# A two-block transformer kernel: grouped-query stage laid out anew, probabilities scaled before transposing, last feed-forward by tokens

## Chip, cores and metric

One core of a Trainium2 chip runs the whole program. The metric is device time in microseconds of one execution, lower is better. Times before are three executions; the profile is of one more.

## The reference, cut to what matters

```
x: (1, 256, 1024) float32
x = x + mixed(rms_norm(x)) @ w_out           # stick-breaking attention, conv, ssm
x = x + cross_attention(rms_norm(x), mem)     # 4 heads of 256
x = x + swiglu(rms_norm(x))                   # feed-forward 0, hidden 2816
x = x + [latent attention (8 heads), dilated attention (3 groups x 4)] @ w_out_ab
x = x + swiglu(rms_norm(x))                   # feed-forward 1
q = rope(rmsnorm(h @ w_q)); k = rope(rmsnorm(h @ w_k)); v = h @ w_v    # 16 q heads, 4 kv heads of 64
x = x + softmax(q k^T / 8) v @ w_o            # grouped-query stage
x = x + swiglu(rms_norm(x))                   # feed-forward 2
return rmsnorm(x, final_norm)                 # y = x * rsqrt(mean(x^2) + eps) * gain
```

## The kernel before

x stays on chip as `xT`, features on partitions, 8 tiles of 128x256. Each engine has its own instruction stream, written out by hand in order, and semaphores tie them together: an engine does its work strictly in the order written. All weights come in pieces of 128x2048 float32 (1 MB) through three `raw` buffers. ACT copies a piece to `whi` in a reduced float32 form, half a piece at a time, and DVE subtracts to get the rest, `wlo` (L764 and L1337 outside the feed-forwards, L1140 and L1722 inside). `split` does one such half; `after(name, idx)` does the splits of the piece whose buffer tile (name, idx) has freed. Each product of a projection is three matmuls: hi x hi, hi x lo, lo x hi (L1949 to L1951 with weights stationary, L2009 to L2011 and L2500 with activations stationary).

A projection tile takes 24 matmuls of 256 columns into one of four PSUM banks in turn (`Plan.tile`, `ring_bank`); `claim` waits until the earlier tile of the same bank is evacuated. Helper `plain` (L2015) issues unsplit float32 matmuls, each of which the profile shows as two records; `pe.transpose` (L2616, L2646) shows as one.

Attention: PE makes scores, DVE takes row maxima, ACT exponentiates and sums, PE turns the probabilities, ACT copies them out, PE multiplies by values, ACT and DVE split the result in hi and lo. In `attend` (cross and latent attention) and in the dilated attention DVE writes a diagonal matrix of reciprocal sums into `hf` (L1702, L1880), and PE turns and scales in one plain float32 matmul against it. In `attend_pairs` (grouped-query) DVE scales the probabilities of two heads (L1330 after L1925) and PE uses `pe.transpose`.

Grouped-query stage: two key tiles are projected side by side, then eight query tiles, each followed in PE's order by the sum of squares of the pair before (`sum_squares`, inside the pair) and by the rotation product (`g_swapped`) of that pair; DVE does for each pair splits, the rotation of the pair before, mean square, scaling (`g_norm`). The value tiles come last, then the last rotation, and only then the first scores; before the first turn PE issues 14 matmuls that nobody reads (`keep_clock`, 28 records).

Feed-forward: a chunk is 256 of 2816 hidden channels. `hidden` makes gate and up (pairs of L2376, 512 columns, and L2378, 256 columns, 16 pairs per half chunk), `output` multiplies a half chunk by its w_out rows into banks 4 to 7 (24 matmuls of 256 columns). Before the first chunk of each, `add_residual` adds the eight tiles of the projection before to xT on DVE, ACT and DVE split the normed x, POOL adds the squares (L732 to L738), and `norm_sum` sums them on PE. After feed-forward 2 the tiles are added to xT, multiplied by the final gain (`final`), squared, summed by columns, transposed to tokens, scaled and stored by one DMA of 1 MB.

## Time and profile before

| what | us |
|---|---|
| median of 3 runs (lowest, highest) | 1214.98 (1212.34, 1221.14) |
| profiled execution, its own time | 1219.0 |
| span from first to last instruction in it | 1217.0 |
| PE busy in it | 1142.1 |
| DVE busy | 836.9 |
| ACT busy | 621.9 |

The profile is of a separate execution, whose own time is 4.0 us over the median of the three; 2.0 us of its time lie outside its span. Busy time of PE is the union of its pipelined matmuls, so that a busy PE may still be given work faster. What is read in it are places: where PE waited, for whom, and the rate at which it worked where it didn't wait.

### The profile page before, as it was taken

The numbers are of one execution on the slowest core, as the hardware profiler recorded it, in microseconds if no ns is written. First come the engines' busy times: TensorE is split into PE (matmuls) and PEld (weight loads), VectorE is DVE, ScalarE is ACT, GpSimd is POOL, SyncE is SP. The second block draws the span as 40 slices with busy tenths as digits, with TensorE's granted clock in tenths as the row PEclk, the third lists the DMA queues.
The fourth block names the chain that finished last, engine by engine and source line by source line (L and its number), as shares of the span: only waits on it lengthen the run. The fifth ranks groups of instructions, "written<-read, shape, count | busy, mean of one in ns | idle before, by whom it ended". The sixth has DMA issues, their size and how long they took to land.

```text
span 1217.0 us, 20958 instructions
## 1 busy us (share of the span) xinstructions
PE 1142.1 (94%) x8064; PEld 1022.6 (84%) x8064; DVE 836.9 (69%) x1291; ACT 621.9 (51%) x1106; POOL 39.5 (3%) x40
## 2 busy tenths in 40 slices
PE   4899899898999999999999989999988799999998
PEld 4787678798989999999977879999987678999997
DVE  3685674456378787777466378787876667778784
ACT  4633445545455455565354455454564565555453
POOL 2000000010010000010000010000010001000000
PEclk8898899999999999999999999999999899999998
DMA  8342222326165567646421056567586205567650
GB/s 256 105 139 82 92 71 69 104 70 190 53 212 175 168 182 207 182 152 201 133 88 35 29 163 178 163 194 207 174 166 143 71 11 166 175 169 206 192 153 36
DMA packets 218145, 169.20 MB, mean 139 GB/s; under 512 B 20787, under 2 KB 208098, under 8 KB 217954
## 3 DMA queue, kind: packets, MB, share of 16 engines
q1 hardware_dynamic: 216962, 164.44, 46.2%
q0 software_dynamic: 496, 2.43, 0.6%
q10 hardware_dynamic: 624, 1.44, 0.4%
q8 instruction: 46, 0.75, 0.3%
q14 instruction: 17, 0.14, 0.0%
HBM read 167.24 MB, written 1.05 MB: 138 GB/s over the span
## 4 chain that ended last, share of the span: by engine, by line
PE 77%; DVE 11%; ACT 7%; issue 2%; SPq 1%; DMA 1%; POOL 0%; POOLq 0%; DVEq 0%; ACTq 0%
PE bank L2376 19%; PE bank L2015 14%; PE bank L1949 10%; PE bank L1950 10%; PE bank L1951 10%; PE bank L2378 10%; DVE wlo L1337 4%; ACT whi L764 2%; DVE arena L1330 2%; PE bank L2009 1%; PE bank L2010 1%; PE bank L2011 1%; ACT arena L1285 1%; SPq L695 1%; DVE hf L1348 1%
## 5 line engine op out<-in xcount | busy, mean ns | idle before, releaser
L2376 PE MATMUL bank<-mem_pair,whi 128*128 128x512 f32 x1056 | 376.4, 399 | 2.5 <-DVE mem_pair L1647 1.6
L2378 PE MATMUL bank<-mem_pair,wlo 128*128 128x256 f32 x1056 | 296.5, 281 | 0.0
L1949 PE MATMUL bank<-act_hi,whi 128*128 128x256 f32 (+1 forms) x920 | 266.0, 289 | 12.7 <-DVE act_lo L1356 4.7
L1950 PE MATMUL bank<-act_lo,whi 128*128 128x256 f32 (+1 forms) x920 | 262.6, 285 | 0.0
L1951 PE MATMUL bank<-act_hi,wlo 128*128 128x256 f32 (+1 forms) x920 | 262.2, 285 | 0.0
L2376 PEld LDWEIGHTS bank<-mem_pair,whi 128*128 128x128 f32 x1056 | 198.5, 188 | 49.6 <-DVE mem_pair L1647 2.7
L1337 DVE TENSOR_TENSOR wlo<-raw,whi 128x1024 fp32r<-128x1024 f32 (+3 forms) x137 | 163.3, 1234 | 103.8 <-ACT whi L764 102.6
L1722 DVE TENSOR_TENSOR wlo<-raw,whi 128x1024 fp32r<-128x1024 f32 x177 | 208.8, 1220 | 4.0
L2378 PEld LDWEIGHTS bank<-mem_pair,wlo 128*128 128x128 f32 x1056 | 199.6, 189 | 0.1
L1949 PEld LDWEIGHTS bank<-act_hi,whi 128*128 128x128 f32 (+1 forms) x920 | 176.8, 192 | 23.7 <-issue 13.0
L1140 ACT ACTIVATE whi<-raw 128x1024 fp32r<-128x1024 f32 x180 | 179.9, 1046 | 0.4 <-PE bank L1951 0.4
L1950 PEld LDWEIGHTS bank<-act_lo,whi 128*128 128x128 f32 (+1 forms) x920 | 177.2, 193 | 0.8 <-issue 0.7
L1951 PEld LDWEIGHTS bank<-act_hi,wlo 128*128 128x128 f32 (+1 forms) x920 | 177.2, 193 | 0.0
L1155 ACT ACTIVATE arena<-arena 128x256 f32<-128x256 f32 x66 | 27.6, 418 | 253.7 <-DVE arena L1330 253.7
L2015 PE MATMUL bank<-arena 32*32 32x256 f32 (+9 forms) x1052 | 134.3, 387 | 17.7 <-ACT arena L1285 4.9
L1746 DVE TENSOR_REDUCE arena<-bank 128x256 f32<-128x512 f32 x132 | 90.6, 686 | 75.8 <-PE bank L2378 75.8
L764 ACT ACTIVATE whi<-raw 128x1024 fp32r<-128x1024 f32 (+3 forms) x134 | 129.5, 1018 | 18.1 <-PE bank L1951 18.1
L2015 PEld LDWEIGHTS bank<-arena 32*32 32x32 f32 (+5 forms) x1052 | 82.7, 136 | 54.3 <-issue 13.2
L1330 DVE TENSOR_TENSOR arena<-arena 128x256 f32<-128x256 f32 (+5 forms) x190 | 95.3, 503 | 40.3 <-ACT arena L1159 21.3
L1949 PE MATMUL bank<-mem_pair,whi 128*128 128x256 f32 (+1 forms) x352 | 106.2, 302 | 2.2 <-DVE mem_pair L1647 2.2
L1950 PE MATMUL bank<-mem_pair,whi 128*128 128x256 f32 (+1 forms) x352 | 101.0, 287 | 0.0
L1951 PE MATMUL bank<-mem_pair,wlo 128*128 128x256 f32 (+1 forms) x352 | 100.8, 286 | 0.0
(216 smaller groups left out, 1330.4 us busy)
## 6 DMA issues: line engine op xcount, KB each, us to landing
raw<-in_ffn_w_in_dram SPq DMA_DIRECT2D x132, 512.0 KB, 5.1
raw<-in_ffn_w_out_dram SPq DMA_DIRECT2D x33, 1024.0 KB, 5.0
raw<-in_w_in_ab_dram SPq DMA_DIRECT2D x11, 1024.0 KB, 5.4
raw<-in_w_in_dram SPq DMA_DIRECT2D x9, 1024.0 KB, 6.2
raw<-in_xa_wk_dram SPq DMA_DIRECT2D x4, 1024.0 KB, 5.7
raw<-in_xa_wv_dram SPq DMA_DIRECT2D x4, 1024.0 KB, 5.2
raw<-in_w_out_dram SPq DMA_DIRECT2D x4, 1024.0 KB, 5.2
raw<-in_xa_wq_dram SPq DMA_DIRECT2D x4, 1024.0 KB, 5.2
```

What stands on the lines that cost most here:

```text
L764: act.activation(whi[g % SLOTS][:, h * n:h * n + n], raw[g % SLOTS][:, h * n:h * n + n], ACT.Copy)\
L1140: act.activation(whi[slot][:, h * 1024:h * 1024 + 1024], raw[slot][:, h * 1024:h * 1024 + 1024], ACT.Copy).then_inc(s_split_hi, 1)
L1330: return dve.tensor_tensor(dst, a, b, ALU.mult)
L1337: dve.tensor_tensor(wlo[g % SLOTS][:, at_], raw[g % SLOTS][:, at_], whi[g % SLOTS][:, at_].bitcast(F32), ALU.subtract).then_inc(s_split_lo, 1)
L1722: dve.tensor_tensor(wlo[slot][:, at_], raw[slot][:, at_], whi[slot][:, at_].bitcast(F32), ALU.subtract)\
L1746: dve.tensor_reduce(x[:, j, :], bank[2 * j + g][:].rearrange("p (h t) -> p t h", h=2), AX.X, ALU.add)\
L1949: pe.matmul(dst, w[0], a[0], start=start, stop=False, **kw)
L1950: pe.matmul(dst, w[0], a[1], start=False, stop=False, **kw)
L1951: return pe.matmul(dst, w[1], a[0], start=False, stop=stop, **kw)
L2015: return pe.matmul(dst, w, a, start=start, stop=stop, skip_group_check=True)
L2376: pe.matmul(b[:].rearrange("p (h t) -> p h t", h=2), w[0][:, k, g, :], mem_pair[:, :, k, :], start=k == 0, stop=False, skip_group_check=True)
L2378: last = pe.matmul(b[:, 0:T], w[1][:, k, g, :], mem_hi[:, k, :], start=False, stop=k == KC - 1, skip_group_check=True)
```

## The change

The diff has some 900 lines. It does the following.

1. Grouped-query stage. The tiles get banks by name, six in all (0 to 3, 5, 6). The sums of squares and rotation products are issued from hooks inside later query tiles. The key pair's squares and the x statistics are taken while the first query tile runs; the first scores come before the value projection, `g_sum(4)` and `g_swapped(3)` lie inside the two value tiles, and `g_swapped(4)` behind the third scores. `keep_clock` is gone. DVE does the last scaling and two rotations between attention steps; the splits for gqa_wo 1 and 2 move to the end of, and behind, the attention.
2. Cross, latent and dilated attention: DVE multiplies the probabilities by the reciprocal sums in place (128x512 at once, or 128x768 twice for the dilated one), and PE uses `pe.transpose`. In cross attention the last query pair is normed inside the first attention steps, and its piece's split comes behind the attention; so does the split after the latent value tiles, behind the dilated attention.
3. `add_residual` and `residual_in` leave the splits after tiles 5 and 7 to the end in all four places (before in one).
4. Feed-forwards: in the first chunk the first half's hi and lo of the hidden come before the splits.
5. Feed-forward 2 works by tokens in its down projection: `x_by_tokens` puts x into banks 4 to 7 (16 plain 128x128 matmuls against the identity), and `output_tokens` accumulates 12 matmuls of 512 columns per half chunk with the hidden stationary. ACT squares and sums each bank, makes the scale, DVE multiplies by it and by the gain, three DMAs store. The final gain is loaded late by POOL, broadcast to 128 partitions (512 KB written), and no longer with the rows at the start.

```diff
-    p.tile("gk", 0, "dve")
-    p.tile("gk", 1, "dve", ("gkv", 0))
-    for j in range(4):
+    p.tile("gk", 0, "dve", None, 0)
+    p.tile("gk", 1, "dve", ("gkv", 0), 1)
+    for j, (b0, b1) in enumerate(((2, 3), (5, 6), (0, 1), (2, 3))):
         p.piece(("gq", j))
-        p.tile("gq", 2 * j, "dve")
-        p.tile("gq", 2 * j + 1, "dve", ("gq", j))
+        p.tile("gq", 2 * j, "dve", None, b0)
+        p.tile("gq", 2 * j + 1, "dve", ("gq", j), b1)
     p.piece(("gkv", 1))
-    p.tile("gv", 0, "act")
-    p.tile("gv", 1, "act", ("gkv", 1))
+    p.tile("gv", 0, "act", None, 5)
+    p.tile("gv", 1, "act", ("gkv", 1), 6)
     residual(p, "gqa_wo")
...
-            sp.wait_ge(s_fine, 4)
-            sp.dma_start(out[0].rearrange("(t p) d -> p t d", p=P), y_tok).then_inc(s_store, 16)
-            sp.wait_ge(s_store, 16)
+            by_token = out[0].rearrange("(t p) d -> p t d", p=P)
+            sp.wait_ge(s_fine, 2)
+            sp.dma_start(by_token[:, 0, :], y_tok[:, 0, :]).then_inc(s_store, 16)
+            for half in range(2):
+                sp.wait_ge(s_fine, 3 + half)
+                at_ = slice(512 * half, 512 * half + 512)
+                sp.dma_start(by_token[:, 1, at_], y_tok[:, 1, at_]).then_inc(s_store, 16)
+            sp.wait_ge(s_store, 48)
 
...
+            pool.dma_start(final_gain, ins["final_norm_2"].rearrange("(a n) -> a n", a=1).to_broadcast([P, D])).then_inc(s_gain, 16)
...
-            rms_from(("xq", 3))
-            after("xq", 7)
...
-            attend(0, 4, probs, probsT, XA_UNITS)
-            residual_in(3, "xa_wo")
+            attend(0, 4, probs, probsT, XA_UNITS, lambda: rms_from(("xq", 3)))
+            after("xq", 7)
+            residual_in(3, "xa_wo", (5, 7))
             x_rms_of(3)
...
+                        early = first and j == 0
+                        if early:
+                            hidden_hi(i, j)
...
-            ffn_tail(1, 6)
+            ffn_tail(1, 6, lambda: pair_squares("gk", "g", 0, 4, split_last=False))
             x_rms_of(6)
-
-
-            for i, j in enumerate(G_ORDER):
-                pair_squares("gq" if j < 4 else "gk", "g", 2 * j if j < 4 else 0, j,
-                             (("g", G_ORDER[i - 1]), 512) if i else None)
-            rms_from(("g", G_ORDER[-1]), 512)
+            rms_from(("g", 4), 512)
+            after("gk", 1)
             x_rms_columns(6)
-            for i in range(2):
-                evacuate("gv", i, gv[:, i, :], scale=x_rms_col[:, i, 0:1])
+            for i in range(1, 5):
+                if i > 1:
+                    rms_from(("g", G_ORDER[i - 1]), 512)
+                pair_squares("gq", "g", 2 * i - 2, G_ORDER[i], split_last=i < 4)
+
+            def gv_out(t):
+
+                evacuate("gv", t, gv[:, t, :], scale=x_rms_col[:, t, 0:1], follow=False)
+
             def attend_pairs(first, pairs):
 
                 for i in range(pairs + 3):
+                    if i == 1:
+                        rms_from(("g", G_ORDER[4]), 512)
+                        gv_out(0)
+                        after("gq", 7)
+                        gv_out(1)
                     for half in range(2):
...
-            act.wait_ge(s_ss, SQ["norm", 8] + 4)
-            step(act.activation(x_rms_col[:], bank[4][:, 0:4].rearrange("p (t k) -> p t k", t=2), ACT.Ln,
-                                scale=1.0 / D, bias=eps[:, 0:1]))
-            act.activation(x_rms_col[:], x_rms_col[:], ACT.Exp, scale=-0.5).then_inc(s_col, 1)
-            act.wait_ge(s_col, 3)
+
+
             for t in range(TT):
-                act.wait_ge(s_fint, 2)
-                act.activation(y_tok[:, t, 0:512], bank[2 * t][:], ACT.Copy, scale=x_rms_col[:, t, 0:1]).then_inc(s_fine, 1)
+                for half in range(2):
+                    act.wait_ge(s_fin, 2 * t + half + 1)
+                    act.activation(sq[:, half, :], bank[4 + 2 * t + half][:], ACT.Square,
+                                   accum_out=final_sums[:, t, half:half + 1]).then_inc(s_mean, 1)
+                act.wait_ge(s_mean, 4 * t + 1)
+                act.activation(final_scale[:, t, :], final_sums[:, t, 0:1], ACT.Identity, scale=1.0 / D, bias=eps[:, 0:1])\
+                   .then_inc(s_mean, 1)
+                act.wait_ge(s_mean, 4 * t + 3)
+                act.activation(final_scale[:, t, :], final_sums[:, t, 1:2], ACT.Ln, scale=1.0 / D, bias=final_scale[:, t, :])\
+                   .then_inc(s_mean, 1)
+                act.wait_ge(s_mean, 4 * t + 4)
+                act.activation(final_scale[:, t, :], final_scale[:, t, :], ACT.Exp, scale=-0.5).then_inc(s_scale, 1)
...
-                        for t in range(TT):
-                            last = dve.tensor_scalar(rescale(a, t), ident, rsum[:, a, t:t + 1], None, ALU.mult)
-                        last.then_inc(s_p, 1)
+                        mul(probs_[:, a % 2, :, :], probs_[:, a % 2, :, :],
+                            rsum[:, a, :].unsqueeze(2).to_broadcast([P, TT, T])).then_inc(s_p, 1)
+                    if middle is not None:
+                        middle(i)
                     if i >= 4 and out_units[i - 4] is not None:
...
-                dve.wait_ge(s_dexp, 2 * s + 2)
-                step(dve.reciprocal(rsum[:, 28 + s, :], rsum[:, 28 + s, :]))
                 for t in range(TT):
-                    last = dve.tensor_scalar(dil_rescale(s, t), ident, rsum[:, 28 + s, t:t + 1], None, ALU.mult)
-                last.then_inc(s_dp, 1)
+                    dve.wait_ge(s_dexp, 2 * s + t + 1)
+                    step(dve.reciprocal(rsum[:, 28 + s, t:t + 1], rsum[:, 28 + s, t:t + 1]))
+                    d = dprobs2[:, s % 2, t, :]
+                    dve.tensor_scalar(d, d, rsum[:, 28 + s, t:t + 1], None, ALU.mult).then_inc(s_dp, 1)
...
+            g_mean(0)
+            g_scaled(0)
+            after("gk", 1)
+            for i in range(1, 4):
+                g_mean(i)
+                after("gq", 2 * i - 1)
+                g_scaled(i)
+                g_rotate(i - 1)
+
             def attend_pairs(first, pairs):
 
+                def scale_pair(a):
+
+                    dve.wait_ge(s_exp, a + 2)
+                    step(dve.reciprocal(rsum[:, a:a + 2, :], rsum[:, a:a + 2, :]))
+                    pr = gprobs[:, a % 4:a % 4 + 2, :, :].rearrange("p h l m -> p (h l) m")
+                    r = rsum[:, a:a + 2, :].rearrange("p h l -> p (h l)")
+                    mul(pr, pr, r.unsqueeze(2).to_broadcast([P, 2 * TT, T])).then_inc(s_p, 2)
+
                 for i in range(pairs + 4):
+                    if i == 1:
+                        g_mean(4)
+                        scale_pair(first)
+                        g_scaled(4)
+                        g_rotate(3)
                     if i < pairs:
                         for a in range(first + 2 * i, first + 2 * i + 2):
                             dve.wait_ge(s_score, a + 1)
...
-                    if 1 <= i <= pairs:
-                        a = first + 2 * i - 2
-                        dve.wait_ge(s_exp, a + 2)
-                        step(dve.reciprocal(rsum[:, a:a + 2, :], rsum[:, a:a + 2, :]))
-                        pr = gprobs[:, a % 4:a % 4 + 2, :, :].rearrange("p h l m -> p (h l) m")
-                        r = rsum[:, a:a + 2, :].rearrange("p h l -> p (h l)")
-                        mul(pr, pr, r.unsqueeze(2).to_broadcast([P, 2 * TT, T])).then_inc(s_p, 2)
+                    if 2 <= i <= pairs:
+                        scale_pair(first + 2 * i - 2)
+                    if i == 2:
+                        g_rotate(4)
                     if i >= 4:
                         c = i - 4
                         dve.wait_ge(s_ohi, OHI[8 + c])
                         dve.tensor_tensor(act_lo[:, c, :], bank[6 + c % 2][:, 0:T], act_hi[:, c, :].bitcast(F32),
                                           ALU.subtract).then_inc(s_olo, 1)
+                    if i == pairs:
+                        after("gq", 7)
 
             attend_pairs(12, 8)
+            after("gv", 1)
             add_residual("gqa_wo", 7)
...
-            dve.wait_ge(s_col, 3)
+            dve.wait_ge(s_gain, 16)
             for t in range(TT):
-                dve.wait_ge(s_fint, 2)
-                dve.tensor_scalar(y_tok[:, t, 512:D], bank[2 * t + 1][:], x_rms_col[:, t, 0:1], None, ALU.mult)\
-                   .then_inc(s_fine, 1)
+                dve.wait_ge(s_scale, t + 1)
+                for half in range(2):
+                    at_ = slice(512 * half, 512 * half + 512)
+                    dve.scalar_tensor_tensor(y_tok[:, t, at_], bank[4 + 2 * t + half][:], final_scale[:, t, :],
+                                             final_gain[:, at_], ALU.mult, ALU.mult).then_inc(s_fine, 1)
 
 
...
-                                last = plain(turned_bank(a)[:, m * T + l * P:m * T + l * P + P],
-                                             probs_[:, a % 2, l, m * P:m * P + P], rescale(a, l))
+                                last = pe.transpose(turned_bank(a)[:, m * T + l * P:m * T + l * P + P],
+                                                    probs_[:, a % 2, l, m * P:m * P + P], ident)
...
+                def output_tokens(j, value, hidden_value, end=False):
+
+                    pe.wait_ge(s_split_lo, value)
+                    pe.wait_ge(s_fflo, hidden_value)
+                    w = [x[os_][:, j * D:j * D + D] for x in (whi, wlo)]
+                    for t in range(TT):
+                        for half in range(2):
+                            b, of, to = bank[4 + 2 * t + half], slice(t * P, t * P + P), slice(512 * half, 512 * half + 512)
+                            plain(b[:], hid_hi[:, j, of], w[0][:, to], False, False)
+                            plain(b[:], hid_hi[:, j, of], w[1][:, to], False, False)
+                            last = plain(b[:], hid_lo[:, j, of], w[0][:, to], False, end)
+                            if end:
+                                last.then_inc(s_fin, 1)
+                    if not end:
+                        last.then_inc(tile_done, 1)
+
+                def x_by_tokens():
+
+                    pe.wait_ge(s_rms, 2 * stat_no["norm", n] + 1)
+                    for c in range(KC):
+                        for t in range(TT):
+                            at_ = slice((c % 4) * P, (c % 4) * P + P)
+                            plain(bank[4 + 2 * t + c // 4][:, at_], xT[:, c, t * P:t * P + P], ident, c % 4 == 0, False)
+
+                step = output_tokens if f == 2 else output
+
                 def chunk(i, first=False, last=False):
...
-            for i, j in enumerate(G_ORDER[1:]):
-                for k in range(2):
-                    project("gq", 2 * j + k, ("gq", j), P * k, XN)
-                    if k == 0:
-                        if i == 0:
-                            norm_sum(6)
-                        sum_squares(("g", G_ORDER[i]), 0, bank[4][:], 2, True, True, blocks)
-                        if i == 1:
-                            x_rms_columns(6)
-                g_swapped(i)
-            for t in range(TT):
-                project_tokens("gv", t, ("gkv", 1), t, XN)
-                if t == 0:
-                    sum_squares(("g", G_ORDER[-1]), 0, bank[4][:], 2, True, True, blocks)
-            g_swapped(4)
+            GQ_HOOKS = ({4: lambda: g_sum(0), 6: lambda: norm_sum(6)}, {4: lambda: x_rms_columns(6)},
+                        {4: lambda: g_sum(1)}, {4: lambda: g_swapped(0)},
+                        {4: lambda: g_sum(2)}, {4: lambda: g_swapped(1)},
+                        {4: lambda: g_sum(3)}, {4: lambda: g_swapped(2)})
+            for n in range(8):
+                project("gq", n, ("gq", n // 2), P * (n % 2), XN, hooks=GQ_HOOKS[n])
...
-                if tile == 0:
-                    evac_wait(pe, "gv", 1)
+                if tile < 2:
+                    evac_wait(pe, "gq", 5 + 2 * tile)
...
-                            keep_clock(SOFTMAX_FILL, 6)
+                            g_swapped(4)
+                            evac_wait(pe, "gv", 1)
...
+            gqa_scores(0, (score_bank(12), score_bank(13)))
+            project_tokens("gv", 0, ("gkv", 1), 0, XN, hooks={4: lambda: g_sum(4)})
+            project_tokens("gv", 1, ("gkv", 1), 1, XN, hooks={2: lambda: g_swapped(3)})
```

## Rows read from the trace of the kernel before

**Rows 1.** Part 2 of the page: TensorE's granted clock in 40 slices.

```profile
PEclk8898899999999999999999999999999899999998
```

**Rows 2.** Busy by stretch: length, PE, PEld, DVE, ACT, POOL, clock.

```profile
687.00:722.00 35.00, 31.44 (x219) 28.28 (x218) 23.35 (x37) 18.07 (x29) 5.49 (x4) 1.00 0.40 121
908.00:959.00 51.00, 39.83 (x268) 32.71 (x268) 34.95 (x48) 25.19 (x48) 0.00 (x0) 0.99 0.62 151
959.00:991.00 32.00, 28.86 (x207) 20.47 (x208) 20.70 (x35) 23.69 (x80) 0.00 (x0) 0.91 0.01 2
```

**Rows 3.** Timeline of PE in the third feed-forward (start us, us, what).

```profile
1106.74 0.40 PE L2376 MATMUL bank<-mem_pair,whi 128*128 128x512 f32 x1
...
1112.38 0.28 PE L1949 MATMUL bank<-act_hi,whi 128*128 128x256 f32 x1
...
1115.26 0.40 PE L2376 MATMUL bank<-mem_pair,whi 128*128 128x512 f32 x1
```

**Rows 4.** The chain that ended last, at the latent value projection.

```profile
627.40 2.74 PE bank L2500 x12
```

**Rows 5.** Timeline of PE, cross attention ([idle before it <- what ended it]).

```profile
303.53 2.08 PE L2015 MATMUL bank<-hf,arena 128*128 128x128 f32 x8 [3.67 <-DVE hf L1702]
...
308.81 1.20 PE L2015 MATMUL bank<-hf,arena 128*128 128x128 f32 x8
```

**Rows 6.** Timeline of DVE at the same place.

```profile
298.74 2.36 DVE L1337 TENSOR_TENSOR wlo<-raw,whi 128x1024 fp32r<-128x1024 f32 x2
```

**Rows 7.** Timeline of PE, latent attention, two heads.

```profile
638.52 1.06 PE L2015 MATMUL bank<-hf,arena 128*128 128x128 f32 x8
639.50 2.14 PE L2015 MATMUL bank<-arena 128*64 128x256 f32 x8
641.48 1.06 PE L2015 MATMUL bank<-hf,arena 128*128 128x128 f32 x8
```

**Rows 8.** Timeline of PE, dilated attention, slots 0 and 1.

```profile
658.45 3.00 PE L2015 MATMUL bank<-hf,arena 128*128 128x128 f32 x24 [1.42 <-DVE hf L1880]
...
666.90 3.00 PE L2015 MATMUL bank<-hf,arena 128*128 128x128 f32 x24
```

**Rows 9.** Timeline of PE, entries of the second and third feed-forward.

```profile
708.17 0.51 PE L2376 MATMUL bank<-mem_pair,whi 128*128 128x512 f32 x1 [1.61 <-DVE mem_pair L1647]
...
712.60 0.70 PE L2015 MATMUL bank<-x_sum,ones 128*128 128x256 f32 x2 [1.00 <-POOL x_sum L738]
...
1027.06 0.36 PE L1949 MATMUL bank<-act_hi,whi 128*128 128x256 f32 x1 [0.89 <-DVE act_lo L1767]
```

**Rows 10.** Timeline of PE, grouped-query stage.

```profile
917.28 1.13 PE L2015 MATMUL bank<-arena 128*128 128x512 f32 x2 [2.18 <-DVE arena L1348]
...
958.81 2.08 PE L2015 MATMUL bank<-arena 64*128 64x256 f32 x8 [4.92 <-ACT arena L1285]
960.82 5.12 PE L2015 MATMUL bank<-ones 128*128 128x128 f32 x28
...
972.32 1.06 PE L2616 MATMUL bank<-cst,arena 128*128 128x128 f32 x8
973.32 2.15 PE L2015 MATMUL bank<-arena 128*64 128x256 f32 x16
975.61 0.63 PE L2616 MATMUL bank<-cst,arena 128*128 128x128 f32 x4
```

**Rows 11.** Groups by line, 966 to 985 us (busy us, mean ns of one).

```profile
L1285 ACT ACTIVATE arena<-bank,nmax 128x256 f32<-128x256 f32 x24 | 11.0, 471 | 6.7 <-PE bank L2616 6.3
...
L1330 DVE TENSOR_TENSOR arena<-arena,rsum 128x1024 f32<-128x1024 f32 x5 | 6.1, 1225 | 0.5
L1294 ACT ACTIVATE arena<-bank 128x512 f32<-128x512 f32 x11 | 6.1, 611 | 0.0
```

**Rows 12.** The chain from the last down projection on.

```profile
1203.77 0.87 PE bank L2015 x8
```

**Rows 13.** SP's waits in the last 17 us.

```profile
SPq L286 <- DMA out_dram<-arena: 3.6, 1, 3.6
```

More of the change, by code:

```diff
@@ L68, in __init__ @@
         self.bank_no = {}
+        self.bank = {}
         self.evac = {}
@@ L2598, in attend_pairs @@
             def attend_pairs(first, pairs):
-                for i in range(pairs + 3):
+                for i in range(1, pairs + 3):
                     if i < pairs:
```

196 lines of the change are left out of this document (102 added, 94 removed).

## The prediction, made before the result was known

> **What bounds the kernel now.** I read the granted clock by slices first, then the busy table by stretch, then PE's timeline where its busy share falls, and at each gap what ended it. The clock is near its upper level (2.4 GHz; the lower is 1.2) nearly everywhere [rows 1]. In the feed-forwards PE has no gap. Its rate there is seen from starts, since the records overlap: 16 pairs of hidden take 1112.38 - 1106.74 = 5.64 us, 0.353 a pair, and 24 matmuls of 256 columns take 2.88 us, 0.120 each [rows 3]. So the kernel is bound by PE's stream, and time can be saved in three ways: fewer or cheaper PE instructions, gaps removed between stages, and the tail after the last projection. The gaps are large in the grouped-query stage: 51.0 us with 39.8 busy, then 32 us at a mean clock of 0.91 [rows 2]. The whole span has 1217.0 - 1142.1 = 75 us without PE.
>
> **Price of a turn.** A plain 128x128 float32 matmul costs 0.98 / 4 = 0.245 us (a head's four, from 638.52 to 639.50 [rows 7]). Eight transposes take 973.32 - 972.32 = 1.00 us, 0.125 each [rows 10]. So four turns fall from 0.98 to 0.50 us.
>
> **Grouped-query stage.** PE's idle before: 11.2 us in 908 to 959 [rows 2], of which 2.2 wait for the scaled keys and 4.9 for the first exponentials [rows 10]. Removed in attention: keep_clock, 965.8 - 960.8 = 5.0 us at the lower clock; 1.0 us since the scores before it (958.81 to 960.82) took twice what 8 such records take in 1.0; and about 1.2 us of waiting right behind. That is 18.4 us at most. What comes in place, going through the new order: the key squares are taken at about 909.3 before the ACT split, so the first sum fits into query tile 0. ACT then has a split (2.0), the x statistics (1.4), the key's Ln and Exp (1.3) and another split before the squares of the first query pair, which are ready some 0.8 us after PE asks for them in tile 2; later hooks have slack (about 1.5 us each; a split pair on DVE is 2.4 [rows 6]). PE's work from the end of the keys to the end of the values is 240 x 0.12 = 28.8, ten sums and rotations at about 0.45, small ones 0.4 and the first scores 1.0, thus about 34.7 us plus 0.8. The first exponentials run under the value tiles. Then the attention is bound by ACT: 972.32 to 975.61 is 3.29 us a pair [rows 10], against four exponentials at 0.45, two copies at 0.5 and an output of 0.4, 3.2 us; DVE has two maxima (1.3), reciprocal and scaling (0.3 + 1.2) and one low part (0.4), also 3.2 [rows 11]. Into this full DVE queue the change puts g_rotate(4), 2.2 us, while ACT's next exponentials wait: I charge 1.5. The split for gqa_wo 1 on DVE at the end (2.4) delays the last low parts by 0.2. gqa_wo 2 is split behind the attention, and covered by four projection tiles of 2.9 us; without that cover it would cost its 2.4. Sum: 18.4 - 0.8 - 1.5 - 0.2 = 15.9; following the order gives 17.2. I take 16.5, with bounds 9 and 19.
>
> **Cross attention.** PE waits 3.67 us [rows 5], because DVE does a split of 2.36 [rows 6] before it takes the first maxima. That split is moved behind the attention; the last norm goes between maxima. In my order the first turn starts near 299.9 instead of 303.5. Behind this wait the clock was at its lower level: eight turn records last 2.08 us [rows 5], and 1.06 in latent attention [rows 7]. The stretch from 303.53 to 308.81 therefore holds 2.6 us too much. Four heads' turns save 1.9. Against it: DVE's scaling of 128x512 is half of the 128x1024 one, plus overhead, 0.7 instead of 0.5 us, and two waits of some 0.3. Gain 3.6 + 2.6 + 1.9 - 0.7 = 7.4 us; 4 if the clock falls all the same.
>
> **Latent attention.** A head is 641.48 - 638.52 = 2.96 us of unbroken PE [rows 7], turns 0.98 of it. With 0.50 it is 2.5. ACT has two exponentials, a copy and half an output, 0.9 + 0.6 + 0.3 [rows 11]; DVE a maximum 0.7, reciprocal 0.2, scaling 0.7, half a low part 0.2. Both stay at 1.8. The first two turns wait for the scaling, so six or seven heads gain 0.5 each: 3.5. **Dilated attention.** PE waits 1.42 us at its start [rows 8] behind the split that is now moved to the end (on DVE it lies beneath the first tile of w_out_ab; uncovered it would cost 1.8); of that 1.1 goes. A slot is 8.45 us [rows 8], with 24 records of turns, 2.93. Twelve transposes are 1.5, but the third group waits for the copy of the first (two banks): 1.8. Gain 4 x 1.1; DVE's two scalings of 768 take longer than two of 128, which costs in the last slot 0.2, and the moved ACT split 0.4 there. Gain 3.5 + 1.1 + 3.8 = 8.4 us.
>
> **Entries of the feed-forwards.** The second waits 1.6 for the x split and 1.0 for POOL's squares [rows 9], since DVE is held by the splits after tiles 3 and 5. In 687 to 722, the output projection up to the first output matmul, PE shows 35.0 - 31.4 = 3.6 us idle [rows 2]; as a gap begins only when the pipelined matmul before it ends, each of the four costs 0.28 more, 4.7. With the late splits and the early hidden all of it goes, but the first reduction of chunk 0 is then held by the late splits for 0.9: 3.8. The first has one such wait of 0.7 and one before its first output, and gains 1.5. In the third the wait before the first output is 0.89 [rows 9], 1.06 us over PE's step; it goes. What is late next is the second half's hidden: some 1.3 us later, of a slack of 2.6.
>
> **Feed-forward 2 by tokens.** x_by_tokens adds 16 x 0.245 = 3.9 us on PE's path, less the 1.06 gap: +2.9. An output falls from 24 x 0.120 = 2.88 to 12 matmuls of 512. Twelve of that form, activations stationary, took 2.74 [rows 4]; as the wide one of a hidden pair it would be 0.353 - 0.120 = 0.233, 2.80. 22 outputs gain 1.8 to 3.1; I take 2.5. The hidden as stationary needs the same semaphores.
>
> **Tail.** Before, from 1203.77 [rows 12] to the span's end, 13.2 us. After, from the last matmul: two squares of a bank on ACT, the second 0.65 us behind the first, about 1.65; three small steps 0.9; DVE two multiplications 1.4; then a 256 KB store instead of 1 MB. The wait for 1 MB was 3.6 us [rows 13]; a quarter in size gives 0.9 if all is transfer, 3.6 if none; I take 2.1 and 0.4 for the issue. 6.5 us; gain 6.7, bounds 5 and 8. The late gain load (POOL's queue has nothing behind it) has 170 us to land.
>
> **Start.** One row DMA less on SP, whose last landing the chain waits for: 0.3 (0 to 0.6).
>
> **Sum** against the profiled execution's 1219.0: 16.5 + 7.4 + 8.4 + 3.8 + 1.5 - 2.9 + 2.5 + 6.7 + 0.3 = 44.2, so 1174.8. The median is 4.0 lower: 1171.
>
> **A rule against it.** In grouped-query attention, a third of whose PE work is transposes, the clock came back and stayed high: after about 965 us no fall is seen until the tail [rows 1, 2]. The Trainium skill says (TensorE: Matmul & The Clock Gate, Part 4: PE-mode transpose) that transposes don't count as PE activity for the clock. If the clock fell for that, each stage with turns would run at half. By the rows the sum stands.
>
> **Rivals.**
> (a) The grouped-query stage keeps half its waits: DVE and ACT do their lists strictly in order, and with splits of 2.4, rotations of 2.2 and scalings of 0.9 a round, one late hook passes on to the next. For it: DVE is filled to 3.2 of 3.29 us in attention. Against: a projection pair lasts PE 6.7 us, and DVE's round is 6.2. Then the gain there is 9: 1179. Chance 0.20.
> (b) The cheaper turns only uncover DVE: exponentials, then scaling, then turn, in latent, cross and dilated attention; 8.4 + 1.9 give 4: 1177. Against: PE has 2.5 us a head, DVE 1.8. Chance 0.12.
> (c) Slower: transposes let the clock fall in cross, latent and dilated attention and in the grouped one. PE's 48 us of latent and dilated work would cost 48 more, cross 8, grouped 20: 1247. It decides from 44 us of lost time on, nearly all those stages. Chance 0.03.
> (d) The order doesn't take effect since the landing of weights sets the pace: gqa_w_q pieces have 256-byte runs. They had landed by 910 before, needed at 915. Gain left only in tail and turns, 15 or less: 1200 to 1208; chance 0.03.
> The forecast has 0.62. The range reaches 8 lower, where the order in grouped-query works out fully (19), tail 8 and outputs 3.1, and to 1188, (a) and (b) together with the low tail: 1161 to 1188. Within 1% is about what a measurement can tell from nothing. Faster by over 1%: 0.94; within: 0.03; slower 0.03.
>
> **What would show it.** PE's rows in the stage of the grouped queries: no gap over 1 us from the keys to the first turn; 3.3 us a pair after. A latent head at 2.5 us, a slot at 7.3. First output of each feed-forward without a gap; output in chunks of feed-forward 2 near 2.75. The tail 6.5 us. I'd be wrong by a clock at its lower level in any attention stage, by PE waiting for DVE's scalings, or by a pair period above 3.5.

## The result and the profile after

The changed kernel takes 1175.15 us (median of 4, 1169.1 to 1177.42), the kernel before 1214.35 in the same comparison: a ratio of 0.966, 95% interval 0.9607 to 0.9713. The forecast was 1171 in a range of 1161 to 1188. The profiled execution took 1177.42 us, its span 1175.3, so that it stands 41.7 under the profiled one before (44.2 forecast).

Cut at the first PE record of each stage, the two traces give this (us; "forecast" is the sum of the terms of the prediction for the stage):

| stage | before | after | measured | forecast |
|---|---|---|---|---|
| mixing, up to the first cross scores (not changed, but for one load) | 293.65 | 295.57 | +1.92 | -0.3 |
| cross attention, to xa_wo | 24.83 | 16.90 | -7.93 | -7.4 |
| xa_wo and feed-forward 0 | 214.01 | 213.33 | -0.68 | -1.5 |
| projections of latent and dilated | 92.95 | 92.95 | 0 | 0 |
| latent attention, to the first dilated turn | 33.01 | 28.67 | -4.34 | -4.6 |
| dilated attention | 28.81 | 24.95 | -3.86 | -3.8 |
| w_out_ab and feed-forward 1 | 211.16 | 207.57 | -3.59 | -3.8 |
| grouped-query stage, to gqa_wo | 92.23 | 75.78 | -16.45 | -16.5 |
| gqa_wo and feed-forward 2, to its last matmul | 212.96 | 212.71 | -0.25 | +0.4 |
| tail | 13.39 | 6.87 | -6.52 | -6.7 |

This table is the instrument of all that follows. In the 14 profiled executions of this study the projection stage, which no kernel changed, lasted 92.93 to 92.96 us, while the mixing stage lasted 287.56 to 297.31. The mean clock of the first 287 us was 0.92 in the profile after, 0.93 before and 0.95 in the run `gqa_only` below. Most of the spread between executions sits there, in falls of the clock. Where the clock doesn't fall, a stage length tells differences of 0.1 to 0.2 us. Where it falls it tells less: cross attention in its old form took 24.83, 24.83, 24.86 and 25.10 us in four profiles, the old tail 11.43 to 13.39. A median of whole executions doesn't tell 2.

The granted clock after (part 2 of the page) shows the same; what answers to [rows 1] has its falls in the first 10 slices and none behind:

```profile
PEclk8998889989999999999999999999999999999999
```

The grouped-query stage by stretch (length, PE, PEld, DVE, ACT, POOL, clock), against [rows 2]: first keys to first scores, then scores and values to gqa_wo. The clock, 0.91 before in the attention, is 1.00 in both.

```profile
879.94:919.00 39.06, 37.73 (x268) 33.18 (x268) 29.81 (x44) 24.05 (x42) 4.72 (x4) 1.00 0.85 180
919.00:955.72 36.72, 32.60 (x241) 22.65 (x239) 30.90 (x50) 29.48 (x93) 0.00 (x0) 1.00 0.10 20
```

PE's timeline after (start us, us, what, idle before):

```profile
301.63 0.66 PE L2387 MATMUL bank<-cst,arena 128*128 128x128 f32 x4
302.51 1.97 PE L2080 MATMUL bank<-arena 128*128 128x256 f32 x8 [0.22 <-DVE arena L1371]
...
357.05 0.36 PE L2009 MATMUL bank<-act_hi,whi 128*128 128x256 f32 x1 [0.30 <-DVE act_lo L1770]
...
628.62 0.60 PE L2387 MATMUL bank<-cst,arena 128*128 128x128 f32 x4
629.16 2.14 PE L2080 MATMUL bank<-arena 128*64 128x256 f32 x8
631.13 0.60 PE L2387 MATMUL bank<-cst,arena 128*128 128x128 f32 x4
...
711.20 0.36 PE L2009 MATMUL bank<-act_hi,whi 128*128 128x256 f32 x1 [0.20 <-DVE act_lo L1770]
...
926.77 3.05 PE L2080 MATMUL bank<-arena 64*128 64x256 f32 x18
929.66 1.04 PE L2709 MATMUL bank<-cst,arena 128*128 128x128 f32 x8
930.65 1.13 PE L2080 MATMUL bank<-arena 64*128 64x256 f32 x8
933.05 1.06 PE L2709 MATMUL bank<-cst,arena 128*128 128x128 f32 x8 [1.26 <-ACT arena L1312]
934.04 2.15 PE L2080 MATMUL bank<-arena 128*64 128x256 f32 x16
937.39 1.06 PE L2709 MATMUL bank<-cst,arena 128*128 128x128 f32 x8 [1.20 <-ACT arena L1312]
...
940.67 1.06 PE L2709 MATMUL bank<-cst,arena 128*128 128x128 f32 x8
...
991.22 3.73 PE L2080 MATMUL bank<-cst,xT 128*128 128x128 f32 x32
994.70 0.47 PE L2080 MATMUL bank<-whi,act_hi 128*128 128x512 f32 x1
...
1003.19 0.40 PE L2080 MATMUL bank<-whi,act_hi 128*128 128x512 f32 x1
...
1005.94 0.39 PE L2441 MATMUL bank<-mem_pair,whi 128*128 128x512 f32 x1
```

To be seen in it: the wait of [rows 5] ahead of the first cross turn is gone. A latent head is 631.13 - 628.62 = 2.51 us ([rows 7]: 2.96). The gap before the first output of each feed-forward is gone, but in the first two feed-forwards a small one stands before the second output (357.05, 711.20). A pair of grouped-query heads takes 940.67 - 937.39 = 3.28, except for one of 4.34 (933.05 to 937.39); that one is over the 3.5 which the prediction named as a sign of being wrong. The rotation that it had charged for makes it (run 4). An output by tokens is 2.75 (1003.19 to 1005.94), x_by_tokens 3.48.

### The profile page after: what moved, and what is told of

It reads as the page before. It is cut to its first block, busy times and chain, and to the rows that moved or that the text cites. A ratio compares the mean times of both kernels' runs of the same rounds, so it can differ in the third digit from the quotient of the medians.

```text
span 1175.3 us, 20129 instructions
## 1 busy us (share of the span) xinstructions
PE 1118.8 (95%) x7660; PEld 988.1 (84%) x7660; DVE 839.6 (71%) x1277; ACT 618.3 (53%) x1104; POOL 39.2 (3%) x41
## 3 DMA queue, kind: packets, MB, share of 16 engines
HBM read 167.76 MB, written 1.05 MB: 144 GB/s over the span
## 4 chain that ended last, share of the span: by engine, by line
PE 80%; DVE 9%; ACT 7%; issue 2%; SPq 1%; DMA 1%; POOLq 0%; POOL 0%; DVEq 0%; ACTq 0%
PE bank L2441 19%; PE bank L2080 17%; PE bank L2009 10%; PE bank L2443 10%; PE bank L2010 9%; PE bank L2011 9%; DVE wlo L1360 2%; DVE arena L1353 2%; PE bank L2074 2%; PE bank L2076 2%; PE bank L2075 2%; ACT whi L766 1%; SPq L691 1%; ACT arena L1303 1%; DVE wlo L1756 1%
## 5 line engine op out<-in xcount | busy, mean ns | idle before, releaser
L2009 PE MATMUL bank<-act_hi,whi 128*128 128x256 f32 (+1 forms) x744 | 216.5, 291 | 10.5 <-DVE act_lo L1379 4.7
L2010 PE MATMUL bank<-act_lo,whi 128*128 128x256 f32 (+1 forms) x744 | 212.9, 286 | 0.0
L2011 PE MATMUL bank<-act_hi,wlo 128*128 128x256 f32 (+1 forms) x744 | 212.8, 286 | 0.0
L2009 PEld LDWEIGHTS bank<-act_hi,whi 128*128 128x128 f32 (+1 forms) x744 | 143.8, 193 | 20.5 <-issue 13.2
L2010 PEld LDWEIGHTS bank<-act_lo,whi 128*128 128x128 f32 (+1 forms) x744 | 144.0, 193 | 0.8 <-issue 0.7
L2011 PEld LDWEIGHTS bank<-act_hi,wlo 128*128 128x128 f32 (+1 forms) x744 | 144.0, 194 | 0.0
```

The costliest lines, as they stand in the source:

```text
L2009: pe.matmul(dst, w[0], a[0], start=start, stop=False, **kw)
L2010: pe.matmul(dst, w[0], a[1], start=False, stop=False, **kw)
L2011: return pe.matmul(dst, w[1], a[0], start=False, stop=stop, **kw)
```

## Experiments

Each is compared by stage with the kernel that it was made from; the ratio is to the kernel before.

**1. The grouped-query stage alone** (`gqa_only`: banks, hooks, order and missing keep_clock put into the kernel before, nothing else).

> The kernel before with the grouped-query stage of the change alone: tile banks by name, hooks, values behind the first scores, no keep_clock; turns, splits, feed-forwards and tail are as before. Theory A, the stage's gain stands by itself: from the first key tile to gqa_wo's first matmul 75.8 us as in the changed kernel instead of 92.2 (before: 898.42 to 990.65), and about 16.4 us off the time, 1198. Rival B, the new order pays only together with the late splits and the cheaper turns around it: under 12 us in the stage, or more than 2 us given back in the residual addition behind it.

1195.8 us, ratio 0.9854 (0.9826 to 0.9882). The stage is 75.80 us, the stages between it and cross attention are those of before to 0.03. Theory A holds. The tail was 1.96 shorter too, 11.43, with no change made there: the mean clock in it was 0.77, and 0.62 in the profile before. The clock fell 3.2 us into the tail in the profile before, 6.2 us into it here. `no_fill` (run 2) shows the same: tail 11.45, clock 0.83, the fall after 7.5 us. So some 2 us of the 6.5 that the tail shows depend on when the clock falls in the old tail.

**2. What keep_clock was worth** (`no_fill`), **and whether transposes bring the clock back** (`fill_transposes`), both in the kernel before; the added lines are those of the second, the first has none:

```
                         if i == 2:
-                            keep_clock(SOFTMAX_FILL, 6)
+                            for _ in range(2 * SOFTMAX_FILL):
+                                pe.transpose(bank[6][:, 0:P], ones[:], ident)
```

> The kernel before without keep_clock: PE waits for the first probabilities instead of issuing 28 records that nobody reads. Theory A, those records did little there, since the clock was already down when they started (957.6) and stood at the lower level until 964.5: the time falls by 0 to 2 us or stays, and PE waits until DVE's first scaled pair. Rival B, they brought the clock back: without them the turns and values behind run at the lower clock for several us, 2 to 5 us slower.

> The kernel before with 28 transposes in place of the 14 plain matmuls (28 records) of keep_clock, so that PE is given as many records. Theory A, transposes bring the clock back as matmuls do: the granted clock rises at about 965 as before, the pair periods behind stay at 3.29 us, time within 1 us. Rival B, transposes don't count for the clock: it stays low for some us longer, the next turns and values take twice their time, 2 to 6 us slower.

Without it: 0.9981 (0.9957 to 1.0006) as a whole, and 87.97 instead of 92.23 us in the stage, 4.26 less. Theory A has the sign and less than half the size; theory B is out. PE in that run:

```profile
959.11 2.08 PE L2015 MATMUL bank<-arena 64*128 64x256 f32 x8 [4.92 <-ACT arena L1285]
961.12 1.97 PE L2616 MATMUL bank<-cst,arena 128*128 128x128 f32 x8
963.02 2.00 PE L2015 MATMUL bank<-arena 64*128 64x256 f32 x8
964.95 1.09 PE L2616 MATMUL bank<-cst,arena 128*128 128x128 f32 x8
```

The first turn starts at once, so the probabilities were ready when the 28 records began: keep_clock held up ready work. Turns and scores last twice their time until about 964.8, where the granted clock rises, and then their own. So 4.26 is less than the fill's own 4.95 us: the low clock stays, and real work runs under it. With transposes as the fill (ratio 1.0002, 0.9976 to 1.0028; stage 92.18) the rise comes as early. PE's timeline, then its busy time and the granted clock by stretch:

```profile
959.63 5.05 PE L2610 MATMUL bank<-cst,ones 128*128 128x128 f32 x28
964.52 1.04 PE L2617 MATMUL bank<-cst,arena 128*128 128x128 f32 x8
965.49 1.13 PE L2015 MATMUL bank<-arena 64*128 64x256 f32 x8
```

```profile
962.00:963.00 1.00, 1.00 (x7) 0.50 0.00 0
963.00:964.00 1.00, 1.00 (x10) 0.84 0.00 0
964.00:965.00 1.00, 1.00 (x12) 1.00 0.00 0
```

28 transposes and nothing else stood between 959.63 and 964.52. Under them the clock goes from 1.2 GHz (0.50) to 2.4, and the eight turns behind last 1.04 us. The Trainium skill (TensorE: Matmul & The Clock Gate, Part 4: PE-mode transpose) says that the high clock doesn't engage for transposes; these float32 ones did not keep it down.

**3. Values behind the first scores** (`values_first`: that order undone).

```
-            gqa_scores(0, (score_bank(12), score_bank(13)))
             project_tokens("gv", 0, ("gkv", 1), 0, XN, hooks={4: lambda: g_sum(4)})
             project_tokens("gv", 1, ("gkv", 1), 1, XN, hooks={2: lambda: g_swapped(3)})
+            gqa_scores(0, (score_bank(12), score_bank(13)))
```

> The changed kernel with the first grouped-query scores issued behind both value tiles, as the kernel before had them; banks, hooks and the orders of ACT and DVE are unchanged. Theory A, a wait of PE for the first exponentials and scaling returns and the clock falls behind it: 4 to 5.5 us of wait at the first turns, then several us at the lower clock, 6 to 10 us in all. Rival B, the wait returns but the clock stays up, since the transposes and scores around it are dense enough: 4 to 5.5 us and a mean clock above 0.97 through the attention. Rival C, the hooks and banks made the gain and this order made little of it: under 2 us.

1175.52 us, ratio 0.9684 (0.9659 to 0.9709): as a whole not to be told from the changed kernel. The stage says otherwise, 81.97 instead of 75.78 us:

```profile
917.51 1.14 PE L2080 MATMUL bank<-arena 64*128 64x256 f32 x8
923.72 5.44 PE L2080 MATMUL bank<-arena 64*128 64x256 f32 x18 [5.07 <-DVE arena L1371]
928.99 1.04 PE L2709 MATMUL bank<-cst,arena 128*128 128x128 f32 x8
```

A wait of 5.07, and 18 records in 5.44 us that take 3.05 with the clock up (926.77 above). Theory A holds; the mixing stage was 8 us shorter in this execution and hid it. Runs 2 and 3 split the stage's gain: 92.23 without keep_clock 87.97, with banks and hooks 81.97, with the values moved 75.78; 4.26, 6.00 and 6.19 us. These are shares in this order of steps, since the last step also removes the low clock that `no_fill` leaves.

**4. The last rotation** (`rotate_pool`: POOL takes two of its three operations; it is idle there).

```
                     if i == 2:
-                        g_rotate(4)
+                        dve.wait_ge(s_rot, 10)
+                        mul(grot, bank7(P, 2), sin_g.unsqueeze(1).to_broadcast([P, 2, T])).then_inc(s_r4, 1)
...
+            pool.tensor_tensor(x4, x4, cos_g.unsqueeze(1).to_broadcast([P, 2, T]), ALU.mult).then_inc(pool_step, 1)
+            pool.wait_ge(pool_step, 6)
+            pool.wait_ge(s_r4, 1)
+            pool.tensor_tensor(x4, x4, grot, ALU.add).then_inc(s_rd, 1)
```

> The changed kernel with the last query rotation shared: DVE multiplies the rotated half by the sines (0.7 us), POOL does the product with the cosines and the addition, which DVE did in 2 x 0.7. Theory A, this rotation in DVE's full queue is what makes the second pair period of the grouped-query attention 4.34 us instead of 3.28: the period falls to 3.3 to 3.6, the stage from 75.8 to about 75.0, and the next scores that need the rotation come before PE asks for them. Rival B, POOL's two operations slow DVE's own while they run, or end too late for the scores of tile 6: the stage stays at 75.8 or grows.

1171.88 us, ratio 0.9634 (0.9586 to 0.9683); the stage 74.78, 1.00 less. PE, and what POOL's operation did to DVE's scaling:

```profile
933.21 1.06 PE L2718 MATMUL bank<-cst,arena 128*128 128x128 f32 x8 [1.27 <-ACT arena L1320]
934.20 2.15 PE L2089 MATMUL bank<-arena 128*64 128x256 f32 x16
```

```profile
930.13 1.27 POOL L749 TENSOR_TENSOR arena<-arena 128x512 f32<-128x512 f32 x1 [41.70 <-PE bank L2089]
933.23 1.27 POOL L752 TENSOR_TENSOR arena<-arena 128x512 f32<-128x512 f32 x1 [1.83 <-DVE arena L1361]
```

```profile
931.07 1.41 DVE L1361 TENSOR_TENSOR arena<-arena,rsum 128x1024 f32<-128x1024 f32 x1
```

The next turns start at 936.50: a pair of 3.29 instead of 4.34. Theory A holds. The scaling that overlapped POOL's first operation by 0.33 us took 1.41 instead of 1.23. The Trainium skill (GPSIMD Engine Reference, 1. Specifications) has the two share their SBUF interfaces and contend when DVE has two SBUF inputs, as here; the trace agrees, with 0.18 us in this one instruction.

**5. Cross attention** (`xa_split_first`: norm and split of the last query pair back ahead of the attention), **and the form of the turn** in cross, latent and dilated attention (`turns_plain`).

```
-                                last = pe.transpose(turned_bank(a)[:, m * T + l * P:m * T + l * P + P],
+                                last = plain(turned_bank(a)[:, m * T + l * P:m * T + l * P + P],
```

> The changed kernel with the last cross-attention norm and the split of the last query piece put back ahead of the attention on ACT and DVE; the turns stay transposes. Theory A, both the wait and the clock return: PE waits 3 to 3.7 us before the first turn, and the turns and values behind it take 2 to 2.6 us more at the lower clock, 5.5 to 6.5 in all. Rival B, the wait returns at the upper clock: 2.4 to 3.7 us. Rival C, the split only moves elsewhere and its place costs nothing: under 1 us.

> The changed kernel with plain float32 matmuls against the identity in place of the transposes in cross, latent and dilated attention; the probabilities are still scaled in place by DVE. Theory A, the form of the turn is the gain there: four turns take 0.98 instead of 0.50 us, a latent head 2.96 to 3.0 instead of 2.50, cross attention 1.9 longer, a dilated slot 8.45 to 8.7 instead of 7.45, in all 8 to 10 us more. Rival B, the turns were covered and the gain came from the scaling in place (DVE no longer writes diagonals): under 3 us more in the three stages together.

Ratios 0.9702 (0.9673 to 0.9732) and 0.9733 (0.9697 to 0.9769). With the split first, cross attention takes 21.86, 4.96 more:

```profile
299.15 1.11 PE L2387 MATMUL bank<-cst,arena 128*128 128x128 f32 x4 [3.88 <-DVE arena L1354]
300.05 2.87 PE L2080 MATMUL bank<-arena 128*128 128x256 f32 x8
302.75 0.60 PE L2387 MATMUL bank<-cst,arena 128*128 128x128 f32 x4
```

From the start of the last scores ahead of the turn to the first turn it is 7.50 instead of 3.47 us, and 0.93 more behind it, at the lower clock until about 302.0: the wait is a little over theory A's, the clock's part under it, and the 4.96 together lie between theory A's 5.5 and rival B's 3.7. With plain turns cross attention is 1.41 longer, latent 3.17, dilated 4.00, 8.6 in all, as theory A has it. A latent head is then 630.54 - 627.57 = 2.97:

```profile
627.57 1.06 PE L2080 MATMUL bank<-cst,arena 128*128 128x128 f32 x8
628.56 2.14 PE L2080 MATMUL bank<-arena 128*64 128x256 f32 x8
630.54 1.06 PE L2080 MATMUL bank<-cst,arena 128*128 128x128 f32 x8
```

What is left of latent attention's gain, 4.34 - 3.17 = 1.17, fits the split that was moved (1.1 forecast): the wait ahead of the first dilated turn, 1.42 in [rows 8], is 0.15 in the changed kernel. In the dilated one 3.86 - 4.00 = -0.14 is left; that this is the dearer scaling is not shown by a run.

**6. The entries of the feed-forwards.** `no_early` puts the first half's hidden behind the splits (`early = False`), `early_both` puts both halves' ahead (`early = first`), `late_before` does the splits of tiles 5 and 7 as before.

> The changed kernel with the first half's hi and lo of the hidden behind the splits again in the first chunk of all three feed-forwards. Theory A, it was this that closed the gap before the first output matmul: 0.6 to 0.9 us more in each of the first two feed-forwards; in the third x_by_tokens (3.5 us) covers it, so nothing there; 1.2 to 1.8 in all. Rival B, the late splits of tiles 5 and 7 closed it: under 0.4 us in all. Rival C, it costs the third as well: over 2.2.

> The changed kernel with the splits after residual tiles 5 and 7 placed as before behind the cross-attention, latent and grouped-query output projections; the early hidden of the first half is kept. Theory A, the late splits made the second feed-forward's gain (the waits of 1.6 and 1.0 us return there: 2.2 us more in that stage, 209.8 instead of 207.6) but cost the first one 0.4 to 0.7 (213.3 falls to 212.9 or less), since the run with the hidden in its old place was 0.7 over the kernel before there. Rival B, the late splits help in both: both stages longer than in the changed kernel.

> The changed kernel with hi and lo of the second half's hidden, too, ahead of the splits in the first chunk. Theory A, the 0.30 and 0.20 us that PE waits before the second output (0.58 and 0.48 with the pipelined end) are all that is left of the entry: each of the first two feed-forwards gains 0.5, and the third nothing, since x_by_tokens covers it. Rival B, the splits that are now later by 0.8 us are waited for by the next hidden or output: no gain, or 0.3 to 1 us lost in each.

| xa_wo and feed-forward 0, w_out_ab and feed-forward 1 (us) | first | second |
|---|---|---|
| before | 214.01 | 211.16 |
| changed | 213.33 | 207.57 |
| `no_early` | 214.73 | 210.37 |
| `late_before` | 212.88 | 210.11 |
| `early_both` | 214.20 | 208.48 |

Ratios: 0.9679 (0.9633 to 0.9725), 0.9679 (0.9643 to 0.9714), 0.9638 (0.9603 to 0.9672), whose differences are within the noise of whole executions. The early hidden is worth 1.40 in the first, more than theory A's 0.6 to 0.9: with the late splits and no early hidden the wait before the first output grows from 0.90 to 1.6:

```profile
346.83 0.36 PE L2009 MATMUL bank<-act_hi,whi 128*128 128x256 f32 x1 [1.61 <-DVE act_lo L1770]
...
702.39 0.36 PE L2009 MATMUL bank<-act_hi,whi 128*128 128x256 f32 x1 [1.76 <-DVE act_lo L1770]
```

In the second, about 1.4 is this gap and 1.4 a fall of the clock behind it: from the first output to the next stage it takes 178.7 us (702.39 to 881.07), where the first feed-forward of the same kernel takes 177.3 (346.83 to 524.12).

```profile
702.39:740.00 37.61, 37.61 (x241) 34.66 (x242) 28.82 (x44) 18.22 (x30) 0.00 (x0) 0.95 0.55 155
```

Whether that fall comes with the wait every time isn't shown; behind 346.83 there was none. With the splits placed as before, the second feed-forward is 2.54 us longer and the first 0.45 shorter, the signs of theory A. But of the two waits that it expected to return only the 1.6 did, and a fall of the clock stood behind it, which the kernel before had not behind the same wait of 1.61 us ([rows 9]; clock 1.00 in [rows 2]). In `late_before`, PE and its busy time by stretch:

```profile
686.33 0.50 PE L2441 MATMUL bank<-mem_pair,whi 128*128 128x512 f32 x1 [1.60 <-DVE mem_pair L1670]
```

```profile
688.00:690.00 2.00, 2.00 (x7) 1.71 (x8) 1.34 (x1) 1.57 (x2) 1.92 (x2) 0.50 1.11 324
```

The clock was low from 687.4 to 690.8. Work of 3.4 us at half speed is a loss of some 1.7 us, an estimate, so that the late splits by themselves are worth about 0.8 of the 2.54 there, and the rest hangs on whether the clock falls. Both halves early costs 0.9 in each, as theory B has it. DVE then does three splits one behind the other ahead of the act_lo that PE waits for:

```profile
359.62 3.50 DVE L1756 TENSOR_TENSOR wlo<-raw,whi 128x1024 fp32r<-128x1024 f32 x3
363.60 0.36 PE L2009 MATMUL bank<-act_hi,whi 128*128 128x256 f32 x1 [1.18 <-DVE act_lo L1770]
```

**7. The store** (`one_store`: one of 1 MB at the end in place of three).

> The changed kernel with one store of 1 MB at the end, behind the last scaling, instead of three. Theory A, the store's time has a part that grows with its size: from the last DVE instruction to the end 3.6 us as before instead of 3.2 (its wait was 2.5 with 256 KB), 0.7 to 1.3 us more in all. Rival B, the wait is a fixed latency and doesn't depend on size: under 0.4 us more. Rival C, the early stores had hidden most of the transfer, which now shows in full: over 2 us more.

Ratio 0.9673 (0.9636 to 0.971); the tail is 2.1 us longer, 8.96. SP's waits in it, then in the changed kernel:

```profile
SPq L288 <- DMA out_dram<-arena: 4.6, 1, 4.6
```

```profile
SPq L288 <- DMA out_dram<-arena: 2.5, 1, 2.5
```

All 2.1 is in the wait for the store, the size of rival C. In the kernel before the same 1 MB took 3.6 [rows 13]; what made it 4.6 here isn't known.

**8. A version from these** (`best`: `rotate_pool`, the splits behind xa_wo as in `late_before`, and the tail's mean by DVE).

> The changed kernel with three edits from the runs so far: the last rotation shared with POOL (1.0 us in the run before), the splits behind the cross-attention output projection placed as before (0.45), and in the tail the mean of the first bank (two instructions of 0.3 us on ACT, which is busy without a gap from the first square to the last scale) computed by DVE, which waits there. Theory A, the gains are in different stages and add: grouped-query stage 74.8, first feed-forward with its projection 212.9, tail 6.5 instead of 7.1; 2.0 us in all, 1173. Rival B, the tail's edit gives nothing, since DVE's mean and the scaling now wait for each other: tail 7.1 or more, 1.4 in all. The difference lies inside what the times of whole executions can tell; the stages in the trace decide.

1173.77 us (median of 6), ratio 0.9641 (0.9605 to 0.9677). Stages: 74.73, 212.78, tail 6.65 (6.87 in the changed kernel): 1.05, 0.55 and 0.2 us less, 1.8 in all. They add. The tail's edit is worth only 0.2; ACT still does its squares of the last two banks one behind the other. By stage it beats the changed kernel; by the median of whole executions this can't be told.

No run undoes the down projection by tokens or the tail's new form as a whole. What is said of them below is read from the rows of the two kernels.

## Why the prediction was right

**The grouped-query stage** (-16.5, measured -16.45) was right in place, and in sum partly by luck: the terms added up to 15.9, following the order gave 17.2, and 16.5 was taken between them. Cut at the first turn, the stage before is 67.35 + 24.88 us (898.42, 965.77, 990.65), and after it is 49.72 + 26.06 (879.94, 929.66, 955.72): 17.63 gained ahead of the first turn, 1.18 lost behind it. Two rows of the kernel before belong to this:

```profile
965.77 1.04 PE L2616 MATMUL bank<-cst,arena 128*128 128x128 f32 x8
969.03 1.06 PE L2616 MATMUL bank<-cst,arena 128*128 128x128 f32 x8 [1.16 <-ACT arena L1294]
```

Three terms of the 18.4 were right. The idle time of 11.2 went but for 0.30. keep_clock took 965.77 - 960.82 = 4.95, charged 5.0; all of it goes, since the low clock goes with it, which `no_fill` alone doesn't do. The scores at the lower clock gave back 1.0. Of the rest four sizes were off. The wait of 1.2 behind keep_clock did not go: it is 1.16 before and 1.26 after (933.05). The six gaps ahead of the first turn were worth some 1.0 more than they show, 0.16 each between the start that PE's step allows and the end of the record before. The wait at the first sum was put at 0.8 and costs 0.46 (0.30 idle). The last rotation was put at 1.5 and costs 1.0. These errors cancelled. Rival (a) has nothing for it: no hook passes a delay on.

**Cross attention** (-7.4, -7.93). From the same scores to the first turn 7.29 us became 3.47, 3.8 (3.6 forecast). From there to xa_wo 14.95 became 10.84; the form of the turn is 1.41 of it by `turns_plain`, so the clock and the scaling are 2.7 (1.9 forecast). The form was put at 1.9: the first turn gains only 0.1, since PE then waits 0.22 for the last norm. **Latent and dilated** (-8.4, -8.20): heads of 2.5, slots of 7.45 where 7.3 was forecast; the third group waits 0.25 for ACT's copy, which the prediction expected. Rival (b) falls: `turns_plain` loses 8.6 us, so the turns weren't covered.

**Entries.** For the second feed-forward 3.8 was forecast and 3.59 came, again with two errors that cancelled. The four gaps were raised from 3.6 to 4.7 us with 0.28 each; by the starts it is 0.16 each, 4.2 (the prediction had it right for the third, 1.06 for a gap of 0.89). And 0.39 and 0.20 us of idle time are left where it kept back 0.9.

For the first, 1.5 was forecast and 0.68 came. Two steps failed. The wait of 0.7 ahead of the first chunk, which the late splits were to remove, is still there. PE before and after:

```profile
342.46 0.47 PE L2376 MATMUL bank<-mem_pair,whi 128*128 128x512 f32 x1 [0.71 <-DVE xT L1654]
```

```profile
336.45 0.47 PE L2441 MATMUL bank<-mem_pair,whi 128*128 128x512 f32 x1 [0.72 <-DVE xT L1677]
```

It is for DVE's addition to xT and not for a split, and it is 0.71 in `late_before` too. And the second half's hidden, said to be 1.3 us later "of a slack of 2.6", had less: PE waits 0.30 for it, 0.47 over its step. With the splits as before (`late_before`) this wait isn't there, so that it is the 0.45 which the late splits cost. The wait before the first output, 0.90 and 1.1 over the step, did go: 1.1 less 0.46 is the 0.68.

**Feed-forward 2 by tokens** (+0.4, -0.25). A turn of x is 3.48 / 16 = 0.22 us, not the 0.245 of a head's four, and the outputs save 0.13 each, 2.9 in 22, where 2.5 was taken. With the gap of 1.06 this makes -0.4; the 0.2 left over are not accounted for. **Tail** (-6.7, -6.52): 6.87 instead of 6.5; the store's wait is 2.5 and not 2.1. Of the gain, 2 us are the early fall of the clock in the profile before (run 1), which the forecast had taken as the tail's own price: luck, as far as the number goes. Against an execution in which the clock fell later the new tail is worth 4.6.

**The 2.5 us between forecast and profile** are 2.2 in the mixing stage (forecast -0.3, measured +1.92), which the change does not touch but for a load, and 0.3 in all others together. The 0.3 for the start can't be told: PE's first record came at 8.04 us before and at 7.71 after, but between 7.70 and 9.14 in the runs made from the changed kernel. The median missed by 4.2, since it was also taken to lie 4.0 under the profiled execution, as before, and lay 2.3 under it. The range was given with more room than its reasons: 2.5 for the grouped-query stage, 1.3 for the tail and 0.6 for the outputs make 4.4 below the forecast, not the 8 that are named, nor the 10 down to 1161. The rule on transposes, rival (c), is out by run 2; nothing waited for a landing, rival (d).

## What to carry to other kernels

Compare stages, not spans: here `values_first`, `no_early` and `no_fill` moved a stage or two by 4 to 6 us and the median by about 1 or less, as an untouched first stage varied by 10. Look at the granted clock in each stage as well: a fall that comes in one execution and not in the next was worth 1.4 to 2 us here. Work that fills a wait to keep the clock must give way when the real work is ready; better is to put real work there, here the value projection behind the first scores (6.2 us, against the 4.3 that leaving out the fill gave). An edit that helps at one entry of a stage can cost at the next one with the same code: measure each place where a shared helper is called.

## What the runs showed of the hardware that was not expected

Behind the wait for the first exponentials the clock came back after 5.7 us of full work in each of three runs, with plain matmuls (964.5), transposes (963.3) or real turns (964.8) in that time alike; in `values_first` it was low for 5.0 us of work and in `xa_split_first` for 2.9. Waits of one size did not do the same to the clock: behind 1.60 us (`late_before`, 686.33) and 1.76 us (`no_early`, 702.39) in an otherwise full stream it fell to the lower level, behind 1.61 us in the kernel before (708.17) and in `no_early` (346.83) it did not. The old tail took 13.4 us at a mean clock of 0.62 and 11.4 at 0.77 and 0.83, in kernels with the same code there; the fall came 3.2, 6.2 and 7.5 us into it. A 1 MB store took 3.6 us in one kernel and 4.6 in another.
